# Writing the queries of the two dilated head groups in residue order, in one hybrid decoder layer

## The reference, cut to what matters

```python
ATTN_GROUPS = ((128, 1), (512, 4), (2048, 16))   # (window, dilation), 4 heads of 64 each
h = rms_norm(x, g_pre_mix); proj = h @ w_in      # q, k, v, pool input, gates
q = apply_rope(q); k = apply_rope(k)
for gi, (window, dilation) in enumerate(ATTN_GROUPS):
    # query t attends keys t - i*dilation, i = 0..window/dilation (128 steps in each group)
    out_g, lse_g = dilated_window_attention(q[hs], k[hs], v[hs], window, dilation)
o_attn = softmax-of-lse-weighted sum of the three groups
merged = sigmoid(gate_a) * (o_attn @ w_proj_attn) + sigmoid(gate_p) * (y_pool @ w_proj_pool)
x = x + rms_norm(merged @ w_out)
x = x + rms_norm((silu(a) * b) @ w_down)         # a, b = halves of rms_norm(x) @ w_gate_up
```

## Time and profile before

| what | value |
|---|---|
| median of 3 runs | 990.07 us (989.28 to 990.28) |
| the profiled execution's own time | 990.13 us |
| its span on the slowest core (core 2) | 988.6 us |
| spans of the eight cores | 983.0 to 988.6 us |
| PE busy | 929.6 us, 94% of the span |
| DVE, ACT, POOL busy | 400.4, 339.7, 277.6 us |

### The profile page before, as it was taken

How to read it: one execution, slowest core, us unless ns; L and a number is a source line. 1 busy time by engine, 2 the same in 40 slices (tenths; PEclk the granted TensorE clock), 3 DMA queues, 4 the chain that set the end, 5 groups by cost and what they waited for, 6 DMA issues and landing times.

```text
span 988.6 us, 15129 instructions; the slowest of 8 cores (983.0 to 988.6 us)
## 1 busy us (share of the span) xinstructions
PE 929.6 (94%) x5422; PEld 464.7 (47%) x5508; DVE 400.4 (40%) x547; ACT 339.7 (34%) x576; POOL 277.6 (28%) x310
## 2 busy tenths in 40 slices
PE   3789999999999999999999999989999999999993
PEld 2455454456664444444544444444444444444441
DVE  3676787856776332233775121111111211111111
ACT  5666640089776222224652111110011111110100
POOL 3543565610001533333663111111331000001231
PEclk9899999999999999999999999999999999999997
DMA  9996425400501631206978766662324445430332
GB/s 242 277 256 167 109 57 136 114 16 3 86 2 44 92 59 22 43 1 177 312 213 173 124 106 122 109 118 62 118 95 128 80 70 86 67 62 10 119 116 76
DMA packets 37482, 105.45 MB, mean 107 GB/s; under 512 B 5792, under 2 KB 5792, under 8 KB 37408
## 3 DMA queue, kind: packets, MB, share of 16 engines
q0 software_dynamic: 15296, 42.05, 25.9%
q1 hardware_dynamic: 19664, 59.26, 18.4%
q10 hardware_dynamic: 2448, 3.18, 1.3%
HBM read 123.43 MB, written 16.78 MB: 142 GB/s over the span
## 4 chain that ended last, share of the span: by engine, by line
PE 82%; DMA 4%; DVE 3%; POOL 3%; ACT 3%; issue 3%; another core or an unknown queue 0%; ACTq 0%; DVEq 0%; POOLq 0%; SPq 0%
PE ps L1276 15%; PE ps L1242 15%; PE ps L1245 15%; PE ps L449 10%; PE ps L561 6%; PE ps L1016 5%; PE ps L1019 5%; PE ps L849 3%; PE ps L871 2%; POOL x1b L1092 2%; PE ps L1023 1%; ACT junk L359 1%; PE ps L1026 1%; DMA xin<-xo 1%; PE ps L424 1%
## 5 line engine op out<-in xcount | busy, mean ns | idle before, releaser
L1242 PE MATMUL ps<-hT,wgu 128*128 128x512 bf16 x659 | 157.6, 379 | 0.7
L1245 PE MATMUL ps<-hT,wgu 128*128 128x512 bf16 x658 | 157.4, 379 | 0.7
L1276 PE MATMUL ps<-wdn,ffT 128*128 128x512 bf16 x689 | 152.8, 382 | 3.5 <-DMA wdn<-wdn 2.6
L1257 DVE TENSOR_TENSOR ffT<-ps,sa 128x512 bf16<-128x512 f32 x88 | 60.8, 691 | 222.5 <-PE ps L1245 212.6
L1256 ACT ACTIVATE sa<-ps 128x512 f32<-128x512 f32 x88 | 52.5, 597 | 239.6 <-PE ps L1242 231.0
L1276 PEld LDWEIGHTS ps<-wdn,ffT 128*128 128x128 bf16 x704 | 69.2, 98 | 87.2 <-issue 5.4
L1245 PEld LDWEIGHTS ps<-hT,wgu 128*128 128x128 bf16 x672 | 65.8, 98 | 79.3
L1242 PEld LDWEIGHTS ps<-hT,wgu 128*128 128x128 bf16 x672 | 65.6, 98 | 78.7
L74 POOL DMA_DIRECT2D wgu<-wgu x42 | 22.6, 537 | 234.6 <-PE ps L1245 215.3
L1092 POOL TENSOR_TENSOR x1b<-tb,xin 128x1024 f32<-128x1024 f32 x31 | 72.8, 2348 | 55.1 <-DVE tb L1087 31.7
L449 PE MATMUL ps<-hT,wqk 128*128 128x512 bf16 x373 | 86.6, 380 | 0.9 <-issue 0.4
(11 more groups left out here) (136 smaller groups left out, 1127.6 us busy)
## 6 DMA issues: line engine op xcount, KB each, us to landing
wgu<-wgu POOLq DMA_DIRECT2D x42, 512.0 KB, 6.3
xst<-xh SPq DMA_DIRECT2D x16, 512.0 KB, 20.0
xin<-xo SPq DMA_DIRECT2D x16, 512.0 KB, 5.4
x1s<-x1b SPq DMA_DIRECT2D x16, 512.0 KB, 3.9
xin<-x1s SPq DMA_DIRECT2D x16, 512.0 KB, 3.9
out<-x1b SPq DMA_DIRECT2D x15, 512.0 KB, 2.9
xst<-xo SPq DMA_DIRECT2D x12, 512.0 KB, 7.7
wdn<-wdn POOLq DMA_DIRECT2D x22, 256.0 KB, 7.2
```

The lines of the kernel that those rows point to most:

```text
L1242: e1 = pe.op(lambda e, k=k, wbuf=wbuf, ba=ba, tok=tok: e.matmul(ps[:, ba, :], lhsT=wbuf[:, 0, k, :], rhs=hT[:, k, tok], start=(k == 0), st ...
L1245: e2 = pe.op(lambda e, k=k, wbuf=wbuf, bb=bb, tok=tok: e.matmul(ps[:, bb, :], lhsT=wbuf[:, 1, k, :], rhs=hT[:, k, tok], start=(k == 0), st ...
L1257: ef = dve.op(lambda e, ub=ub, bb=bb, j=j, b=b: e.tensor_tensor(out=ffT[:, j, b * 512:(b + 1) * 512], in0=ps[:, bb, :], in1=sa[ub][:, :], ...
L1276: ev = pe.op(lambda e, j=j, h2=h2, pr_=pr_, il=il: e.matmul(ps[:, pr_[0] + h2, :], lhsT=ffT[:, j, il * 128:(il + 1) * 128], rhs=wdn[:, j, ...
```

## The change

`q_dst` gives, for the chunks of dilation d = 4 or 16, a view of the whole chunk as d streams of 2048/d positions, and a block of 512 tokens writes 512/d positions into each. The POOL addition at the end of both rope paths reads its two float32 inputs in that order, with a step of d elements. `att_scores` then reads 128 queries side by side for every group, and `qcol` goes. The own keys are written and read as before. The masks, the values, `acc` and the order of the instructions on every engine stay.

```diff
     def q_dst(c, b):
-        return qT[:, c, b * 512:(b + 1) * 512]
+        g = c // 2
+        if g == 0:
+            return qT[:, c, b * 512:(b + 1) * 512]
+        n = 512 // DIL[g]
+        return qT[:, c, :].rearrange("p (r L) -> p r L", r=DIL[g])[:, :, b * n:(b + 1) * n]
...
             i0, i1 = (t.rearrange("p (s j) -> p s j", s=4) for t in (i0, i1))
+        elif g:
+            i0, i1 = (t.rearrange("p (j r) -> p r j", r=DIL[g]) for t in (i0, i1))
         ev_o = pool.op(lambda e: e.tensor_tensor(out=dst, in0=i0, in1=i1, op=ALU.add), waits=[ev_t1, ev_t2])
...
         i0, i1 = t12_t[i][:, 0, :], t2s_t[i][:, :]
+        if g:
+            i0, i1 = (t.rearrange("p (j r) -> p r j", r=DIL[g]) for t in (i0, i1))
         ev_o = pool.op(lambda e: e.tensor_tensor(out=dst, in0=i0, in1=i1, op=ALU.add), waits=[ev_t, ev_sw])
...
         for n, c in enumerate(order):
-            g = c // 2 % 3
-            dst = q_dst(c, b) if c < 6 else k_dst(g, c % 2, HT + b * 512, 512)
-            ew = [wld_ev["w%s%d" % ("q" if c < 6 else "k", g)], [hev[own + 4 * b + t] for t in range(4)]]
+            g = c // 2 if c < 6 else 0
+            dst = q_dst(c, b) if c < 6 else k_dst(c // 2 - 3, c % 2, HT + b * 512, 512)
+            ew = [wld_ev["w%s%d" % ("q" if c < 6 else "k", c // 2 % 3)], [hev[own + 4 * b + t] for t in range(4)]]
...
-    def qcol(g, s_, slot):
-        if g == 0:
-            return slice((4 * s_ + slot) * 128, (4 * s_ + slot + 1) * 128)
-        return slice(512 * slot + s_, 512 * (slot + 1), 4) if g == 1 else slice(4 * s_ + slot, 2048, 16)
-
     def att_scores(u):
...
-            qs = qcol(g, s_, slot)
+            qs = slice((4 * s_ + slot) * 128, (4 * s_ + slot + 1) * 128)
```

## The result

The change takes the median from 989.67 us (4 runs) to 982.04 us (4 runs); the ratio to the kernel before is 0.9929, 95% interval 0.9912 to 0.9946, that is 7.0 us less (5.3 to 8.7). 12.1 us less were forecast. The attention gave about what was forecast; 5 us of it were lost again ahead of its first unit.

A forecast was written before the change was run, and what follows sets the result against it. PE was taken to bound the rope stage and attention. Savings of 8.4 + 1.2 + 2.8, less 0.3 for ACT and 0 for POOL, made 12.1 us: from 990.13 to 978.0 us, range 974.5 to 984.

The forecast's parts named there:

- What bounds, and which operand is slow: Rope stage and attention: PE's stream bounds, so savings reach the end; the strided moving query slows scores, strided weight loads hide.
- Term 1: Scores of dilation 16: 1.07 to 0.45 us a unit, step 2.66 to 2.06 us; 8.4 us saved over 14 steps.
- Term 2: Start of the attention, units 0 to 2: shorter first scores let the third unit start earlier, 1.2 us saved.
- Term 3: Scores of dilation 4: 0.58 to 0.40 us a unit, 2.8 us saved over 16 steps, less 0.3 for ACT.
- Term 4: Rope stage, POOL's 16 strided additions: 1.27 to 1.9 us each, hidden, so cost 0; at most 3 us.
- the slot of 2.24: Rope stage: four dilated query additions in a row start 2.24 us apart, room claimed to cover POOL's 1.9 us.
- the four buffers of the swap path: Rope stage, blocks 2 and 3: buffers claimed to cover POOL's longer additions as the slot does, cost 0.
- The sign that I had named for this case: First scores, expected still at about 200.6 us: a later start would show the forecast wrong through POOL.
- the key rival: Attention scores: strided key loads bound the pairs once queries are quick; dilation 16 at 0.69 us, 983 us, chance 0.12.
- dilation 4 did gain: Dilation-4 scores: the rival said their 0.58 us comes from the keys, so no gain; 980.8 us, chance 0.09.
- POOL's own time never became the bound: Rope stage: the rival had POOL additions at 3.8 us or more, making PE wait; 999 us at 4.5, chance 0.05.
- the last rival: Attention, more gain than forecast: ACT doesn't bind and keys are free; 974.5 us, chance 0.04.

The follow-up runs named there:

- split additions: The change with each strided POOL addition of blocks 2 and 3 issued as two instructions of 256 elements; ratio 0.9901 to the kernel before.
- block 2's new order: The change with block 2 computed in the order 4, 5, 2, 3, 10, 11, 8, 9, 6, 7, 0, 1; ratio 0.9902 to the kernel before.

## Why the prediction was right and wrong

**What bounds, and which operand is slow**: right. PE's stream carried the gain to the end (680.33 and 680.30 us from the start of unit 47 on), and the moving operand was the slow one: with strided keys still there, scores went from 1.07 to 0.39 us.

**Term 1** was too small: 9.4 in place of 8.4 us. I had put 0.12 us on the strided keys; they cost 0.06 (0.39 against 0.33, and 0.33 with sorted keys). And I took the longer of ACT's and PE's time in each step, 2.07 in eleven and PE's 2.04 in three. On core 6 ACT's exponentials start 2.03 to 2.11 us apart in eleven steps and 1.78 to 1.82 in the three in which DVE copies the values, 2.01 as a mean and without idle time; the double buffers average them and take up the 0.2 us that are left over 14 steps, so the step came out at PE's 1.98.

**Term 2** was right in mechanism, 1.2 us: with a punctual start 3.03 us in place of 4.20. In the change itself 3.60 as a mean of the cores, for the clock behind the hole.

**Term 3**: 2.2 in place of 2.5 us. The two parts erred against each other: scores 0.35 and not 0.40, which gives 16 x 0.23 = 3.7, and on core 6 1.4 us of waits (0.34 for DVE, 0.58 and 0.46 for ACT) where I had charged 0.3. The line rule of the Trainium skill (SBUF — State Buffer, Specifications), which I had set against this term, would have given nothing; the runs went with the row, 0.35 us in place of 0.58.

**Term 4 is the step that failed.** The price was right, 1.9 us forecast and 2.0 to 2.13 measured (below), though my argument beside it had a wrong number: 1.27 us for 512 elements is 2.5 ns an element and not 2.1. The conclusion "below the slot of 2.24, so it costs 0: PE's own eight matmuls cover it" held for blocks 0 and 1. "In blocks 2 and 3 the four buffers of the swap path do the same" was wrong. I asked whether POOL keeps up, and not what POOL's longer instructions do to DVE, which waits for them (above) and was at 20.36 and 23.07 us of busy time in 27 and 31 us. The stretched 64x16 row was in the trace of before. Nor did I ask what the clock does behind a hole. Forecast 0, measured +5.0 us at the start (3.4 of waiting, 1.8 of clock, less 0.35 for ACT) and 0.6 in the first units. The terms as measured, 9.4 + 1.2 + 2.2, less those 5.6 come to 7.2, the difference of the spans. The sign that I had named for this case, a later start, is the one that came. The measured time lies below the 984 us that I gave as the upper end, but that end was made of the key rival and "a little POOL"; that it also covers this loss is luck.

**The rivals**: keys didn't take over; dilation 4 did gain; POOL's own time never became the bound in the form that I gave, though it is the engine that cost the 5 us, by another path. ACT didn't bind, as in the last rival, though it never idled in the dilation-16 steps.

## What to carry to other kernels

A strided moving operand of short matmuls is paid on PE (1.07 us against 0.39 for eight), while a strided stationary one is nearly free (0.39 against 0.33); so sort the side that moves, and leave the other. When work is shifted to POOL, look at DVE's instructions with two SBUF inputs in the same stretch, not only at POOL's slack: each that begins during a POOL addition waits until it is over, so place long POOL instructions where DVE reads PSUM. Price a new wait of PE by what the clock does behind it too. Ask also which transfers a moved load will meet. The same change is faster with block 2's dilated queries first (0.9902), with split additions (0.9901) or with both (0.9905, 2.3 us under the change on the same chip).

## What the runs showed of the hardware

A wait of PE of 2.5 to 4.8 us halved its granted clock for the matmuls that followed, and 3.4 us of waiting came to 5.8 us; waits of 0.4 to 1.7 us in the same place, before the change and with block 2's new order, left it at 1.00. In between the length alone didn't decide: with split additions the clock fell on the cores that waited 1.93 and 2.32 us and stayed on one that waited 2.25, and with the new order besides it stayed on one that waited 2.51.

POOL's float32 addition of 512 elements takes 1.27 us with inputs side by side, 2.0 with a step of 64 bytes and 2.13 with one of 16 bytes, so the smaller step is no cheaper; with a strided bf16 write it takes 2.5 to 2.7. The row of core 2 after the change, block 0 (POOL groups, 106 to 112 us, two additions of each step):

```profile
L515 POOL TENSOR_TENSOR qT<-t,t2b 128x512 bf16<-128x512 f32 x4 | 8.2, 2071 | 2.5 <-DVE rsA L404 1.9 <-DVE t2b L500 0.6
```

The Trainium skill, GPSIMD Engine Reference, Performance pitfalls for Q7 kernels, gives half as much again for reads beyond 8 bytes of step; here it is 1.6 to 1.7 times. On TensorE a step of 8 bytes in the moving operand already costs: 0.58 us for eight matmuls against 0.35.
